# A decoder layer on one core: half of the mixer's output projection multiplied inside the stick-breaking stage, and the scan's unused operand in SBUF

## The reference

```
h  = rms(x); [q|k|v|u] = h @ w_in                 # 512 columns each
A: 8 heads x 64, stick-breaking attention, strictly causal:
   a[t,s] = sigmoid(z[t,s]) * prod_{s<j<t} (1 - sigmoid(z[t,j])),  z = q k^T / 8
B: trailing means of u (windows 2, 4, 8, 16) minus the token, a 128x128 map per group, a gain
x += concat(A, B) @ w_out                          # rows 0..511 of w_out for A, 512..1023 for B
x += CrossAttn(rms(x), rms(mem))
```

## Time and profile before

| | |
|---|---|
| three runs | 2016.60, 2017.77, 2019.95 us (median 2017.77) |
| the profiled execution | span 2016.6 us; the page gives no other time of it |
| PE busy | 1974.8 us (98%), 9369 matmuls |
| DVE, ACT, POOL busy | 1328.2, 865.4, 583.3 us |
| granted TensorE clock | 0.996 of full speed on average |
| stick-breaking stage | first score matmuls at 850 us, last values at 994 us |

### The profile page before, as it was taken

How to read it: one execution, slowest core, us unless ns; L and a number is a source line. 1 busy time by engine, 2 the same in 40 slices (tenths; PEclk the granted TensorE clock), 3 DMA queues, 4 the chain that set the end, 5 groups by cost and what they waited for, 6 DMA issues and landing times.

```text
span 2016.6 us, 25198 instructions
## 1 busy us (share of the span) xinstructions
PE 1974.8 (98%) x9369; PEld 1626.8 (81%) x9369; DVE 1328.2 (66%) x1791; ACT 865.4 (43%) x1529; POOL 583.3 (29%) x428
## 2 busy tenths in 40 slices
PE   7999999999999999989999999999999999999998
PEld 6888888887887788766788888888888888878887
DVE  6765565559799732487655555568656556579897
ACT  6534434434445411387634444344443443434444
POOL 1354554530002221065311000221655455410001
PEclk8999999999999999999999999999999999999999
DMA  4223223245500222544134322240322322265102
GB/s 153 78 74 94 84 73 95 84 149 186 187 11 11 68 95 84 148 93 105 42 115 129 113 74 63 63 115 22 105 84 74 94 84 74 73 252 176 63 1 84
DMA packets 217042, 190.15 MB, mean 94 GB/s; under 512 B 7596, under 2 KB 171992, under 8 KB 216920
## 3 DMA queue, kind: packets, MB, share of 16 engines
q1 hardware_dynamic: 216832, 188.51, 30.2%
q10 hardware_dynamic: 88, 0.02, 0.0%
HBM read 152.85 MB, written 35.65 MB: 93 GB/s over the span
## 4 chain that ended last, share of the span: by engine, by line
PE 61%; DVE 4%; ACT 2%; issue 1%; POOL 0%; DVEq 0%; ACTq 0%; POOLq 0%
PE ps L974 19%; PE ps L976 19%; PE ps L975 19%; PE ps L1309 1%; PE ps L1290 1%; DVE rest L2313 1%; PE ps L1276 1%; DVE sr_lo L1895 0%; DVE wb_lo L1895 0%; DVE xn_tmp L1949 0%; PE ps L1280 0%; ACT beta L1781 0%; ACT rest L1762 0%; ACT wb_hi L1461 0%; PE ps L1425 0%
## 5 line engine op out<-in xcount | busy, mean ns | idle before, releaser
L1895 DVE TENSOR_TENSOR w_lo<-st,w_hi 128x512 fp32r<-128x512 f32 x160 | 174.7, 1093 | 177.0 <-ACT w_hi L1461 176.9
L974 PE MATMUL ps<-T_hi,w_lo 128*128 128x512 f32 x640 | 249.7, 390 | 1.2 <-issue 1.1
L975 PE MATMUL ps<-T_lo,w_hi 128*128 128x512 f32 x640 | 249.2, 389 | 0.0
L976 PE MATMUL ps<-T_hi,w_hi 128*128 128x512 f32 x640 | 249.2, 389 | 0.0
L974 PE MATMUL ps<-tr_hi,sr_lo 128*128 128x512 f32 x616 | 242.2, 393 | 3.9 <-DVE tr_lo L1895 3.1
L975 PE MATMUL ps<-tr_lo,sr_hi 128*128 128x512 f32 x616 | 240.1, 390 | 0.0
L976 PE MATMUL ps<-tr_hi,sr_hi 128*128 128x512 f32 x616 | 240.0, 390 | 0.0
L974 PE MATMUL ps<-B_hi,w_lo 128*128 128x512 f32 x576 | 226.4, 393 | 3.5 <-DVE B_lo L1895 2.6
L975 PE MATMUL ps<-B_lo,w_hi 128*128 128x512 f32 x576 | 225.1, 391 | 0.0
L976 PE MATMUL ps<-B_hi,w_hi 128*128 128x512 f32 x576 | 225.1, 391 | 0.0
L974 PE MATMUL ps<-act_hi,wb_lo 128*128 128x512 f32 x384 | 152.4, 397 | 1.7 <-DVE wb_lo L1895 1.6
(11 more groups left out here) (267 smaller groups left out, 4222.8 us busy)
## 6 DMA issues: line engine op xcount, KB each, us to landing
gate_raw<-in_ffn_w_gate SPq DMA_DIRECT2D x44, 512.0 KB, 5.2
up_raw<-in_ffn_w_up SPq DMA_DIRECT2D x44, 512.0 KB, 5.1
h_spill<-up_s SPq DMA_DIRECT2D x66, 256.0 KB, 2.0
piece_A<-in_ffn_w_down SPq DMA_DIRECT2D x32, 512.0 KB, 4.5
piece_B<-h_spill SPq DMA_DIRECT2D x32, 512.0 KB, 6.0
wa_raw<-in_w_in SPq DMA_DIRECT2D x16, 512.0 KB, 4.0
wb_raw<-in_w_out SPq DMA_DIRECT2D x16, 512.0 KB, 3.8
wb_raw<-in_mem_w_kv SPq DMA_DIRECT2D x16, 512.0 KB, 3.8
```

The lines of the kernel that those rows point to most:

```text
L974: pe.matmul(to, w_lo, m_hi, start=first, stop=False, skip_group_check=joins)
L975: pe.matmul(to, w_hi, m_lo, start=False, stop=False, skip_group_check=joins)
L976: return pe.matmul(to, w_hi, m_hi, start=False, stop=last, skip_group_check=joins)
L1895: return dve.tensor_tensor(to, value, plain(hi), ALU.subtract)
```

## The change

The pooled half of the output projection (rows 512 to 1023 of w_out) is taken out of the projection stage and multiplied in steps 5 to 52 of the stick-breaking stage. It is 16 units (8 column tiles, 2 token halves) of four chunks; one unit takes three steps (one chunk, one chunk, two chunks), between the scores and the transposes of the step, in the PSUM bank that was `STILL_BANK` and is now `FILL_BANK`. DVE adds each finished unit to `xT`. The eight weight tiles of 128x512 have a raw buffer of their own and two slots of split weights; SP loads them between the loads of heads, ACT and DVE split them every sixth step. The scan's ignored operand is now an element of `ones`, a constant in SBUF.

The pooled results get tensors of their own (`pl_hi`, `pl_lo`), as does the attention's output (`o_hi`, `o_lo`). In the projection stage only the attention's half is left: tiles are paired, two column tiles of four chunks in one weight slot, so `out0` and `out1` have four tiles each instead of eight. The memory's squares, root and scaling move into the last steps of the stick-breaking stage. Three semaphores are merged into others.

```diff
+        pl_hi, pl_lo = at(108, "pl_hi", [P, NG, SEQ], F32R), at(124, "pl_lo", [P, NG, SEQ], F32R)
+        o_hi, o_lo = at(140, "o_hi", [P, QC, SEQ], F32R), at(156, "o_lo", [P, QC, SEQ], F32R)
+        fw_raw = at(106, "fw_raw", [P, QC, P])
+        fw_hi, fw_lo = at(152, "fw_hi", [P, 2, QC, P], F32R), at(168, "fw_lo", [P, 2, QC, P], F32R)
...
-        B_STEPS = tiles("out0", 0, 1) + [("mem_rms",)] + tiles("out0", 1, 3) + [("memT",)] + tiles("out0", 3, DC)
+        B_STEPS = tiles("out0", 0, 2) + [("memT",)] + tiles("out0", 2, QC)
         for j in range(0, DC, 2):
             B_STEPS += tiles("mk", j, j + 2) + [("tot", 4)] * (j == 0)
-            B_STEPS += tiles("out1", j, j + 1) + [("bc", 4)] * (j == 0)
-            B_STEPS += tiles("mv", j, j + 2) + xn_steps(4, j, j + 1)
-            B_STEPS += tiles("out1", j + 1, j + 2) + xn_steps(4, j + 1, j + 2)
+            B_STEPS += tiles("out1", j // 2, j // 2 + 1) + [("bc", 4)] * (j == 0)
+            B_STEPS += tiles("mv", j, j + 2) + xn_steps(4, j, j + 2)
...
+        FILLS = 2 * DC
+        FILL_FROM, FILL_CHUNKS = TURN_LAG + 1, (0, 1, 2, 4)
+        FILL_STEPS = len(FILL_CHUNKS) - 1
+        def fills_at(step):
+            u, n = divmod(step - FILL_FROM, FILL_STEPS)
+            return range(QC * u + FILL_CHUNKS[n], QC * u + FILL_CHUNKS[n + 1]) if 0 <= u < FILLS else ()
+        def fill_done(step):
+            n = step - FILL_FROM + 1
+            return n // FILL_STEPS - 1 if n > 0 and n % FILL_STEPS == 0 and n <= FILL_STEPS * FILLS else None
+        FILL_TILE_STEPS = FILL_STEPS * 2
+        def fill_weight_at(step):
+            if step == 2:
+                return 0
+            j, off = divmod(step, FILL_TILE_STEPS)
+            return j if off == 0 and 1 <= j < DC else None
...
# SP
+            def fill_load(j):
+                if j == 0:
+                    sp.wait_ge(s_bc, 4)
+                else:
+                    sp.wait_ge(s_mw_lo, j + 1)
+                sp.dma_start(fw_raw[:], w_out[0][SBW:D, j * P:(j + 1) * P].rearrange("(c p) m -> p c m", p=P)
+                             ).then_inc(s_mw_in, 16)
+            fill_load(0)
             for h in range(2, HEADS):
                 stack_load(h)
+                for j in {3: (1, 2, 3), 5: (4, 5), 7: (6, 7)}.get(h, ()):
+                    fill_load(j)
...
# PE
+            def fill(n):
+                u, c = divmod(n, QC)
+                j, half = divmod(u, 2)
+                if c == 0:
+                    if half == 0:
+                        pe.wait_ge(s_mw_lo, j + 2)
+                    if u:
+                        pe.wait_ge(f_add, u)
+                mm = three(ps[:, FILL_BANK, :], fw_hi[:, j % 2, c, :], fw_lo[:, j % 2, c, :],
+                           pl_hi[:, c, tok(half)], pl_lo[:, c, tok(half)], c == 0, c == QC - 1)
+                if c == QC - 1:
+                    mm.then_inc(f_out, 1)
...
+                for n in fills_at(s):
+                    fill(n)
                 if 0 <= s - TURN_LAG < M:
                     turn(s - TURN_LAG)
                 if s == M + 4:
-                    pe.wait_ge(s_scan, M)
+                    pe.wait_ge(f_add, FILLS)
                     tile(B_STEPS[0])
...
# ACT, in step s
+                j = fill_weight_at(s)
+                if j is not None:
+                    act.wait_ge(s_mw_in, 16 * (j + 2))
+                    if j >= 2:
+                        act.wait_ge(f_out, 2 * (j - 1))
+                    copy(fw_hi[:, j % 2], fw_raw[:]).then_inc(s_mw_hi, 1)
...
# DVE
-                dve.tensor_tensor_scan(r[:, ::-1], r[:, ::-1], ps[:, STILL_BANK, 0:1].broadcast_to([P, n]), 1.0,
+                dve.tensor_tensor_scan(r[:, ::-1], r[:, ::-1], ones[:, 0:1].broadcast_to([P, n]), 1.0,
                                        ALU.mult, ALU.bypass).then_inc(s_scan, 1)
...
+                unit = fill_done(s)
+                if unit is not None:
+                    j, half = divmod(unit, 2)
+                    dve.wait_ge(f_out, unit + 1)
+                    dve.tensor_tensor(xT[:, j, tok(half)], ps[:, FILL_BANK, :], xT[:, j, tok(half)],
+                                      ALU.add).then_inc(f_add, 1)
+                j = fill_weight_at(s - 1)
+                if j is not None:
+                    dve.wait_ge(s_mw_hi, j + 2)
+                    lo(fw_lo[:, j % 2], fw_raw[:], fw_hi[:, j % 2]).then_inc(s_mw_lo, 1)
```

More of the change, by code:

```diff
@@ L573, in layer_program, with tiles_made @@
         ADDS = ("out0", "out1", "o0", "o1")
+        PAIRED = ("out0", "out1")
+        def tiles_made(step):
+            return 2 if step[1] in PAIRED else 1
         b_first, b_hi_of, n_units, n_hi = {}, {}, 0, 0
@@ L578, in layer_program @@
             made = {"PV": HD, "tile": 1}.get(step[0], 0)
+            if step[0] == "tile":
+                made = tiles_made(step)
             if step[:2] == ("tile", "mv"):
@@ L613, in layer_program @@
         assert all(end <= 4 for _, end in z_bank)
-        STILL_BANK = a_bank[A_PROJ + 4]
-        TURN_BANKS = [b for b in (4, 5, 6) if b != STILL_BANK]
-        assert STILL_BANK != 7
+        FILL_BANK = a_bank[A_PROJ + 4]
+        TURN_BANKS = [b for b in (4, 5, 6) if b != FILL_BANK]
+        assert FILL_BANK != 7
         def turns(m):
@@ L1339, in tile, with stick_part @@
                     return
+                if kind in PAIRED:
+                    half = int(kind[-1])
+                    def stick_part(i, d):
+                        cols_ = slice(i * P, (i + 1) * P)
+                        return three(ps[:, 4 + (k + i) % 4, :], wide(wb_hi, n % 2)[:, d, cols_],
+                                     wide(wb_lo, n % 2)[:, d, cols_], o_hi[:, d, tok(half)], o_lo[:, d, tok(half)],
+                                     d == 0, d == QC - 1)
+                    if n == 0:
+                        for i in range(2):
+                            if i:
+                                pe.wait_ge(s_aT, copied(M - 1, False))
+                                pe.wait_ge(s_aT_dve, copied(M - 1, True))
+                            for d in range(QC - 1):
+                                stick_part(i, d)
+                        pe.wait_ge(s_o_free, W - 1)
+                        for i in range(2):
+                            stick_part(i, QC - 1).then_inc(b_out, 1)
+                        return
+                    for i in range(2):
+                        if n == 1 and i:
+                            pe.wait_ge(s_o_free, W)
+                        if k + i >= 4:
+                            pe.wait_ge(b_free, k + i - 3)
+                        for d in range(QC):
+                            mm = stick_part(i, d)
+                        mm.then_inc(b_out, 1)
+                    return
                 if k >= 4:
@@ L1342, in tile @@
                 bank = ps[:, 4 + k % 4, :]
[L1344 to L1348, removed]
+                for d in range(DC):
+                    ends = d == 0, d == DC - 1
                     if kind == "o1" and j == 0 and d == HD * (MHEADS - 1):
@@ L1707, in empty @@
                 if step == ("split", 4):
[L1708 to L1709 removed]
+                    act.wait_ge(s_mw_in, 16)
+                    copy(wp_hi[:], wp_raw[:]).then_inc(s_mw_hi, 1)
                 if step[0] == "split":
@@ L1722, in empty @@
                 if kind == "pool":
-                    copy(a_hi_t[part][:, DC // 2 + j, :], bank,
+                    copy(pl_hi[:, j, tok(part)], bank,
                          scale=gains[:, GP + j:GP + j + 1]).then_inc(a_ehi, 1)
@@ L1750, in b_weight @@
                     else:
-                        act.wait_ge(b_out, b_first[before] + (MC if before[1] == "mv" else 1))
+                        act.wait_ge(b_out, b_first[before] + (MC if before[1] == "mv" else tiles_made(before)))
                 copy(wb_hi[:, n % 2], wb_raw[:, n % 2]).then_inc(b_hi, 1)
@@ L1812, in _ @@
                         b_weight(b_tile[step] + 2)
-                    if kind in ADDS:
-                        act.wait_ge(b_free, k + 1)
[L1815 to L1824, removed]
+                    if kind in PAIRED:
+                        for i in range(2):
+                            act.wait_ge(b_free, k + i + 1)
+                            square(4 + int(kind[-1]), 2 * j + i)
+                    elif kind in ADDS:
+                        act.wait_ge(b_free, k + 1)
+                        square(6 + int(kind[-1]), j)
                 elif step[0] == "memT":
@@ L2346, in _ @@
                     b_weight(1)
+                elif s == M + 5:
+                    dve.wait_ge(s_mem_sq, MC + 1)
+                    newton(mvar[:, 1, :], mvar[:, 2, :], [mvar[:, i, :] for i in (3, 4, 5, 6)], s_mem_chain, 1)
+                    for c in range(MC):
+                        dve.tensor_scalar(mem_rows[:, c, :], mem_rows[:, c, :], mvar[:, 6, c:c + 1], None,
+                                          ALU.mult).then_inc(s_mem_scaled, 1)
             for step in B_STEPS:
@@ L2352, in _ @@
```

(10 more changed lines are left out.)

69 lines of the change are left out of this document (38 added, 31 removed).

## The result

The changed kernel takes 2031.35 us (median of 4 runs, 2030.21 to 2031.73), the kernel before 2018.41 (4 runs): ratio 1.0063, interval 1.0049 to 1.0077. It is slower by 13 us, 10 more than forecast and 1.4 us above the range. Its profiled execution has a span of 2029.9 us, 13.3 above the one before.

The account below looks back on a forecast made before the run. It took the stick-breaking stage for an in-order relay of four engines led by PE. Terms: -5.5 (idle filled) + 7.5 (last tiles) + 0.5 (queue, start) + 1.0 (projection), rounded to +3: 2021 us, range 2016 to 2028.

Parts of the forecast that it names:

- the turns: Stick-breaking stage: with two SBUF operands scans alternate with GpSimd's products; 0.8 us a period, 2.4 over three in steps 5 to 52.
- Rival A: Stick-breaking stage: the scan doesn't take turns, so the change is faster, about -7 us, 2011; chance 0.2.
- the last tiles: Last 11 steps, without fills: turns of scans and products aren't covered, +5.8 to +9.2 us, taken as 7.5.
- The fills thus win back 7.9 - 2.4 = 5.5 us: Steps 5 to 52: fills take up 7.9 us of PE's idle time, less 2.4 for turns.
- I add 0 to 2.5, take 1.0: Projection stage: weights' low part and additions queue on DVE behind the memory's transposes, with fewer full tiles following; +1.0 us.
- The queue: Fill weights loaded behind SP's loads of heads: ACT may stop for 0 to 1.5 us, taken as 0.3.
- Rival B: Fill steps: turns pace them too, 3 x 2.7 = 8 us; in all +11, 2029; chance of above +8: 0.24.

Follow-up runs that it names:

- e1: The kernel before with one edit: the scan's ignored operand is an element of ones in SBUF; 2038.98 us, ratio 1.0103.
- e2: Changed kernel with the scan's operand back in PSUM and fills multiplied ahead of the scores in their bank, pooled half left out of the result; 2026.28 us.
- e3: Changed kernel without any fill matmuls, loads, splits or additions, the scan's operand in PSUM; 1982.78 us, ratio 0.983.
- e17: Changed kernel with ScalarE taking up each fill tile's weights 2 to 4 steps before use in place of 5; 2030.64 us, ratio 1.0063.
- e4: Changed kernel with a fill unit's chunks put as two, two, none and its addition one step earlier; 2027.19 us, ratio 1.005.
- e8: Changed kernel with fill units placed anew, two chunks in each of two steps, 10 chunks in the last stretch; 2022.8 us, ratio 1.0024.
- e12: The text doesn't say which edit bears this label; it has the changed kernel's order and slots behind the stage, 152.2 to 154.0 us there.
- the first two reorderings: e7 and e9, two other orders of the tiles after the stage in the changed kernel; 2030.21 and 2030.33 us.
- e7: Changed kernel with long tiles of two column tiles between each pair of mk and mv tiles after the stage; 2030.21 us, ratio 1.0064.
- e9: Changed kernel with the memory's transposes one long tile earlier, then a long tile between pairs of short ones; 2030.33 us, ratio 1.0058.
- e14: Changed kernel with each pair of normalization steps moved ahead of a long tile; 2023.32 us, ratio 1.003.

## Why the prediction was wrong

The direction was the likeliest one, the size wasn't: two of four terms failed. The forecast was +3 us (-2 to +10), measured were +13.

**Right: the turns.** A scan with the idle operand in SBUF alternates with the products. That was concluded from subtractions in the FFN stage, and e1 against the kernel before (a scan over 1024 keys goes from 2.27 to 3.14 us) and the last tiles of e2 against the changed one show it by themselves. Rival A is dead. By the rule of the Trainium skill (SBUF — State Buffer, "Who interferes with whom") the second SBUF operand is what matters; the trace agrees even though the scan's bypass ignores that operand's values: 2.93 us against 2.27.

**Right: the last tiles**, +7.5 forecast, +7.9 measured. The mechanism is shown; that the size came within 0.4 us is partly luck. The sum of scans and products is 32.8 us with the overlaps taken off and 36.2 without, and the text took the middle for want of anything better; the stretch took 34.9. At least 0.6 us of it is a slower TensorE clock, which no term has (last section).

**Failed: "The fills thus win back 7.9 - 2.4 = 5.5 us".** They won 1.8. The text named DVE's copies of transposed blocks as what is late next (they were, by 0.6 us), and left out the wait that the change itself adds: each unit of fills waits until the addition has freed the single bank, and the addition is queued on DVE behind a scan that waits its turn, or in step order behind work that isn't due yet (with no turns at all, in e2, PE still waits 6.9 us for it). That was 7.2 us, nearly the 7.9 us of idle time that there was to win. With the wait taken away, the steps won 4.8 us with turns and 6.7 without: the working, 7.9 less 2.4 for the turns, was about right for a kernel without this wait. The diff shows it (one wait for f_add, at each unit's first chunk).

**Failed: "I add 0 to 2.5, take 1.0" for the projection stage.** It was 7.5 in the marks and 8.3 by e3. The text looked at the memory's transposes; behind them the first short tile starts 0.6 us after the matmul ahead of it, in place of the usual 0.2. It didn't follow the other thing that halving the out tiles does: the normalization's steps lost the long tiles that covered them. This is a cover that the diff takes away without touching a line of the normalization's work.

**The queue.** "ACT may stop for 0 to 1.5 us" was 3.1 and 2.5 us; but as e17 shows at most 0.7 us of it reached the end. Each stop was longer than forecast, the effect on the end about as taken (0.3).

**Rival B** (turns pace the fill steps) came nearest in time, 2029, but its 8 us are not there: with the additions early and the turns in place these steps are about 2 us longer than without turns, and PE waits in them 1.8 us for ScalarE's copies and 1.7 for DVE's, the ones that the forecast names. A total that fits isn't evidence for its story.

**Readings that were off without bearing on the sum.** Of the four engines "each with a share of 70 to 90%" GpSimd has 57% (76.5 of 134 us), and "what lies around the span is taken as nothing" is 1.8 us in every timed profile (2031.69 against 2029.9).

**Open.** The loss behind the stage is one number per profile, and kernels with the same order there spread: 5.2 to 7.0 us where the clock stayed up (e2, e4, e8, e12), 7.5 in the changed kernel and 8.5 in e3. Why the first two reorderings won nothing in sum was read from one trace each, and no run took their own pauses away.

## What to carry to other kernels

When work is moved into an engine's idle time, list the waits that it brings, first of all the buffer that it turns in: with one bank, the operation that frees it has to stand in its engine's order at the earliest place where its input is ready, or the moved work stalls for as much as it should have filled. Then look at the place that it was taken from: long matmul tiles cover relays of other engines (here a normalization), and where they get fewer, those relays must be placed anew. And a scan's ignored operand is not free: in SBUF it makes the scan take turns with GpSimd's products.

## What was not expected of the hardware

TensorE's granted clock fell to 0.50, the level of 1.2 GHz, from 1010.2 to 1017.0 us in the changed kernel, in the last tiles, with PE busy 29.84 of 34.9 us in them, and once more from 1030.7 us on (in the row of the last tiles the mean is 0.86). Ahead of the first fall PE was idle for 2.26 us, up to 1009.41; ahead of the second for no more than 1.23 us, which the kernel before has too, without a fall. The kernel with the operand alone has an idle time of 2.32 us and a fall beside it in every period (0.66 as the mean of 980 to 990 us in its last tiles). The kernel before shows 1.00 in its last tiles at much the same share of busy time, with 1.23 us as its longest idle time there, and so does the kernel with fills spread into them, at 30.95 of 34.6 and again 1.23 us at the longest. The clock fell again at 1109.2, half a microsecond after a pause of 2.05 us ahead of 1108.68: matmuls of 0.63 us, 0.43 apart, up to 1112. In PE's timeline:

```profile
1108.68 0.50 PE L1024 MATMUL ps<-o_hi,wb_lo 128*128 128x512 f32 x1 [1.77 <-DVE wb_lo L1998]
1109.32 0.63 PE L1026 MATMUL ps<-o_hi,wb_hi 128*128 128x512 f32 x1
1109.74 0.63 PE L1024 MATMUL ps<-o_hi,wb_lo 128*128 128x512 f32 x1
```

Seven or so of them cost 0.2 us more each: the tile takes 6.95 us where the others of its kind take 5.34, 1.6 more. Like pauses at 1087 and 1128 us had no such fall behind them, so a pause alone doesn't decide it. In the last tiles the slow clock cost little: e7, e9, e14 and e17, which run the same tiles with some 3 us less of it, took 34.3 us in them against 34.9.
